# A decoder step with product-key experts: dense gates added element by element with indirect DMAs

## The chip, the core and the metric

One core of a Trainium2 chip runs the whole program in one launch. The metric is the device time of one execution in microseconds (us). Engines: TensorE (PE in the profile), VectorE (DVE), ScalarE (ACT), GpSimd (POOL) and SyncE (SP), which here only issues DMAs. 16 DMA engines move data between HBM and SBUF.

## What is computed

Two blocks in a row on 512 tokens of 1024 features, all float32. The first block is a mixing layer (retention and differential attention) followed by a layer of product-key experts; the second is another attention block. The change is in the experts' layer:

```python
def block(xb):                                     # 128 tokens
    q = (xb @ wq).reshape(t, 8, 2, 128)
    s = jnp.einsum('thpd,hpkd->thpk', q, subkeys)  # 128 keys on each side
    s_top, i_top = lax.top_k(s, 16)
    cand = (s_top[:, :, 0, :, None] + s_top[:, :, 1, None, :]).reshape(t, 8, 256)
    c_top, c_idx = lax.top_k(cand, 16)
    i1 = take(i_top[:, :, 0], c_idx // 16); i2 = take(i_top[:, :, 1], c_idx % 16)
    e = i1 * 128 + i2                              # one of 16384 experts
    g = jax.nn.softmax(c_top, axis=-1)
    act = jax.nn.gelu(einsum('thkd,td->thk', u[e], xb))
    return einsum('thk,thkd->td', g * act, v[e])
```

Each token picks 128 experts (8 heads of 16), each with a gate. Two heads can pick the same expert; its gates then add up.

## The kernel before

The experts' layer is computed densely: `hidden` is gelu(u x) for all 16384 experts and all 512 tokens, and for tokens 128 to 511 (`DENSE` = 3 tiles of 128 tokens, `TD` = 384 tokens) it is multiplied by a dense matrix of gates (zero nearly everywhere) and by v. The first tile of 128 tokens is done by rows instead: GpSimd fetches, for each of the 128 picks, one hidden value (`row_unit`) and one row of v (`row`) per token, and VectorE adds them up.

The stages, in the order of each engine's program:

- Mixing and the scores of the keys (0 to 405 us). GpSimd has nothing to do in it. Weights stream through SyncE's queue in pieces of 512 KB with three buffers.
- The hidden layer (`hidden_*`, 128 blocks j of 128 experts, 405 to 1194 us). For each block SyncE loads a piece of u (L1373, four buffers), ScalarE rounds it to `u_high` (L1420), VectorE subtracts to `u_low` (L1449), TensorE makes 24 products of 128x512 (L1398: high times high, high times low, low times high, for 8 slices), ScalarE applies gelu (L1436), SyncE stores 256 KB to `hidden_scratch` in HBM (L1381). Every third hidden buffer must be stored before it is written again.
- Beside it, in units dealt out by `pace(j)`, runs a background: first the choice of the experts on VectorE (`choose_vector`, four token tiles, tiles 1, 2, 3 and then 0), and behind it, from block 64 on, the building of the gates.
- Building the gates: the picked keys and gates of a tile are transposed on TensorE (L1149, behind a wait for `picked`, L1242 on VectorE) and copied by ScalarE (L1169). Then for each of the 384 tokens VectorE makes a 128x128 one-hot matrix of key 1 (L1345) and two of key 2 times the gate's high and low half (L1347), in float16. TensorE multiplies them (L1290, two products of 128x128 per token, in order between the large products), ScalarE moves four tokens at a time from PSUM into a stage (L1312), and six DMAs of 4 MB store them to `gates_scratch` (L1317), 64 tokens each.
- Combining (`combine_*`, 1194 to 1790 us), 32 groups of four key blocks. SyncE loads the gates of a group (`load_gated`, L1478: six DMAs of 128 KB, L1487, and the hidden values, L1489) and v (L1496, 1 MB each, two a group). VectorE multiplies gates and hidden values (L1635), both factors are split in high and low, and TensorE adds three token tiles up in six PSUM banks (L305 to L307). GpSimd fetches rows and units (L1532, L1539), and VectorE adds them to x (L1657).
- The second block (1790 us to the end), untouched.

The hidden layer and the combining overlap by hand: at the blocks of `EARLY` (116, 119, 121, 123, 125, 127) each engine's program goes one step into its `combine_*`. At block 116 SyncE waits for the gates and calls `load_gated(0)`; this stands in SyncE's program between the store of hidden block 116 and the load of u block 121.

Of the kernel before, what the change touches and what calls it, by code (L numbers as in the profile page):

```python
# [13 lines left out]
P = 128  # L14
T = 512
# [62 lines left out]
class Signals:  # L78


    def __init__(self, nc):
# [28 lines left out]
         self.gate_shifted, self.gate_powered, self.picked, self.picked_turned, self.picked_moved) = semaphores(  # L110
            nc, "subkeys_arrived query_act query_dve keys_scored scores_act scores_dve gate_shifted gate_powered "
                "picked picked_turned picked_moved")

        self.hot_parts, self.gates_built, self.gates_moved = semaphores(
            nc, "hot_parts gates_built gates_moved")
        self.gates_stored = semaphores(nc, "gates_stored0 gates_stored1")
# [265 lines left out]
class Mixing:  # L382
    def __init__(self, m, keep):
# [22 lines left out]
        self.small = region.tensor("mix_small", [P, 64], F32)  # L406
        assert region.at <= keep.stream_at
# [502 lines left out]
GATE_BANKS = (4, 5, 6, 7)  # L910
# [3 lines left out]
GATE_CHUNK = 64  # L914
CHUNKS = TD // GATE_CHUNK
HOT = 16
BLOCKS = TD // HOT
COMBINE_BANKS = (4, 5, 6, 7, 0, 1)
ROWS, UNITS = 8, 16

FIRST_ROW = 10
GATE_SCALE = 2.0 ** 15
BATCH = 4
# [9 lines left out]
def pace(j):  # L933
    return 1 + (j % 4 == 3) if j < 64 else 2
# [12 lines left out]
class Peer:  # L947
    def __init__(self, m, keep):
# [4 lines left out]
        self.chosen = [region.tensor(n, [P, TD], dtype) for n, dtype in (("key1", F16), ("key2", F16), ("gate", F32))]  # L953
# [24 lines left out]
        region = Region(nc, self.scores_at)  # L978
        self.stages = [region.tensor(f"gate_stage{i}", [P, N_KEYS, GATE_CHUNK], F32) for i in range(2)]
        self.every_key = region.tensor("every_key", [P, N_KEYS], F16)  # L980
        self.rounded = region.tensor("gate_rounded", [P, TD], F16)
        self.key_values = [region.tensor(f"key_value{i}", [P, TD], F32) for i in range(2)]
        self.parts = [region.tensor(f"gate_part{i}", [P, TD], F32) for i in range(2)]
        self.hot1 = [region.tensor(f"hot1_{i}", [P, HOT, N_KEYS], F16) for i in range(2)]
        self.weighed = [[region.tensor(f"hot2_part{p}_{i}", [P, HOT, N_KEYS], F16) for p in range(2)] for i in range(2)]

# [7 lines left out]
        hot_end = region.at  # L994
        region = Region(nc, self.scores_at)
        self.gate_in = [region.tensor(f"gate_in{i}", [P, CHUNKS, GROUP, GATE_CHUNK], F32) for i in range(2)]
# [7 lines left out]
        region.at = max(region.at, hot_end)  # L1004
        self.unit_places = region.tensor("unit_places", [P, HK], U32)
        self.row_places = region.tensor("row_places", [P, HK], U32)
        self.row_gate = region.tensor("row_gate", [P, HK], F32)
        self.unit = region.tensor("row_unit", [P, HK], F32)
        self.row_weight = region.tensor("row_weight", [P, HK], F32)
        self.place_value = region.tensor("place_value", [P, HK], F32)  # L1010
        self.place_square = region.tensor("place_square", [P, P], F32)
        self.token = region.tensor("token_number", [P, 1], F32)
# [125 lines left out]
def choose_tensor(m, keep, p):  # L1138
    pe, s = m.pe, m.s
    yield  # L1140
    for t in range(TT):
        for _ in range(CHOICE_STEPS + 6):
            yield
        if t < DENSE:
            b = GATE_BANKS[t % 4]
            pe.wait_ge(s.picked, t + 1)
            m.await_bank(b)
            for i in range(3):
                step = pe.engine.transpose(m.bank[b][:, i * P:i * P + P], p.picked[:, i, :], keep.ident[:, :])  # L1149
            step.then_inc(s.picked_turned, 1)  # L1150
            m.bank_freed[b] = (s.picked_moved, 3 * t + 3)
        yield


def choose_scalar(m, keep, p):
    act, s = m.act, m.s
    yield
    for t in range(TT):
        for _ in range(CHOICE_STEPS):
            yield  # L1160
        act.wait_ge(s.gate_shifted, t + 1)
        act.engine.activation(p.picked[:, 2, :], p.picked[:, 2, :], ACT.Exp).then_inc(s.gate_powered, 1)
        for _ in range(6):
            yield
        if t < DENSE:
            b = GATE_BANKS[t % 4]
            act.wait_ge(s.picked_turned, t + 1)
            for i in range(3):
                act.engine.activation(p.chosen[i][:, t * P:t * P + P], m.bank[b][:, i * P:i * P + P], ACT.Copy).then_inc(s.picked_moved, 1)  # L1169
        yield  # L1170
# [18 lines left out]
def choose_vector(m, keep, p):  # L1189
# [5 lines left out]
    for t in range(TT):  # L1195
# [19 lines left out]
        dve.wait_ge(s.picked_turned, t)  # L1215
# [32 lines left out]
        if t == DENSE:  # L1248
            place_rows(m, keep, p)
# [3 lines left out]
def place_rows(m, keep, p):  # L1253
# [4 lines left out]
    dve.wait_ge(s.picked, TT)  # L1258
    dve.step(v.tensor_tensor(p.place_square[:, :], keep.ident[:, :], keep.counting[:, :], ALU.mult))
    dve.settle()  # L1260
    dve.step(v.tensor_reduce(p.token[:, :], p.place_square[:, :], AX_X, ALU.add))
    dve.step(v.tensor_copy(p.row_gate[:, :], gate))
    dve.settle()
    dve.step(v.tensor_scalar(p.unit[:, :], key1, float(T), p.token[:, :], ALU.mult, ALU.add))
    dve.settle()
    dve.step(v.scalar_tensor_tensor(out=p.place_value[:, :], in0=key2, scalar=float(P * T), in1=p.unit[:, :], op0=ALU.mult, op1=ALU.add))
    dve.settle()
    v.tensor_copy(p.unit_places[:, :], p.place_value[:, :]).then_inc(s.places_ready, 1)
# [9 lines left out]
def gates_tensor(m, keep, p):  # L1278
    pe, s = m.pe, m.s
    for _ in range((1 + 4 + 3) * BATCH):  # L1280
        yield
# [1446 lines left out]
```

## Time and profile before

| | us |
|---|---|
| Runs of the kernel | 2227.22, 2224.61, 2226.02 (median 2226.02) |
| The profiled execution | 2222.24, span of the core 2220.8, mean granted TensorE clock 0.975 |

| engine | busy, us | share of the span |
|---|---|---|
| TensorE | 2075.6 | 93% |
| VectorE | 1451.2 | 65% |
| ScalarE | 760.5 | 34% |
| GpSimd | 357.0 | 16% |

The profile is of one execution. L12 is line 12 of the kernel. A group of instructions is a line, an engine and an operation with its tiles. TensorE's products overlap: a 128x512 product shows some 0.39 us, but the next one starts 0.23 us behind it, so the spacing of blocks is the better measure of its rate. GpSimd's spans are rough.

### The profile page before, as it was taken

Reading aid. Unit: us, or ns where it says so; the run is one execution under the profiler, and the core shown is the slowest. Engines: PE = TensorE matmul, PEld = TensorE weight load, DVE = VectorE, ACT = ScalarE, POOL = GpSimd, SP = SyncE. Lnnn points to the kernel's source line nnn. Section 1 sums busy time; section 2 is a strip of 40 time slices with the busy share of each in tenths; the row PEclk is TensorE's granted clock in tenths of the full one; section 3 lists DMA queues with packets and bytes.
Section 4 is the critical chain, followed back from the end, with each engine's and each line's share of the span. In section 5 each row is a group of like instructions: output and inputs, shape, how many; then the busy total and the mean of one; then the engine's idle time right before and its main releaser. Section 6 shows DMA issues by size and latency. Waiting matters only on the chain.

```text
span 2220.8 us, 25836 instructions
## 1 busy us (share of the span) xinstructions
PE 2075.6 (93%) x9641; PEld 1624.8 (73%) x9641; DVE 1451.2 (65%) x3415; ACT 760.5 (34%) x1101; POOL 357.0 (16%) x262
## 2 busy tenths in 40 slices
PE   6989999999999999999999998889789979999899
PEld 5767778878787866666678886677667757777677
DVE  4465442588787978888823576777668864876434
ACT  4334431333232333333333332222223354334531
POOL 0000000000000000000003557577575200000000
PEclk9999999999999999999999999999899989999999
DMA  5211132244443435555576889899889812221022
GB/s 164 84 57 58 57 105 95 95 133 148 133 143 128 147 123 184 188 184 190 190 290 202 274 287 329 311 320 326 282 305 365 319 50 74 76 76 58 19 96 85
DMA packets 172653, 374.90 MB, mean 169 GB/s; under 512 B 19440, under 2 KB 60912, under 8 KB 171504
## 3 DMA queue, kind: packets, MB, share of 16 engines
q1 hardware_dynamic: 146112, 277.03, 37.4%
q0 software_dynamic: 22528, 67.19, 8.1%
q10 hardware_dynamic: 3888, 29.03, 3.2%
q8 instruction: 76, 1.25, 0.2%
q14 instruction: 49, 0.40, 0.1%
HBM read 312.38 MB, written 60.82 MB: 168 GB/s over the span
## 4 chain that ended last, share of the span: by engine, by line
PE 62%; DVE 15%; DMA 7%; issue 6%; POOL 5%; ACT 5%; SPq 0%; ACTq 0%; DVEq 0%
PE bank L1398 27%; PE bank L305 9%; PE bank L307 9%; PE bank L306 9%; DMA v_raw<-in_peer_v 5%; POOL row_unit L1539 5%; DVE x L1657 2%; PE bank L1290 2%; DVE v_low L1646 1%; DMA row<-in_peer_v,row_places 1%; DVE u_low L1449 1%; DVE hidden_in L1635 1%; PE bank L1949 1%; ACT v_high L1596 1%; DVE weights_low L298 1%
## 5 line engine op out<-in xcount | busy, mean ns | idle before, releaser
L1398 PE MATMUL bank<-xn_low,u_high 128*128 128x512 f32 x1024 | 433.8, 424 | 0.0
L1398 PE MATMUL bank<-xn_high,u_high 128*128 128x512 f32 x1024 | 403.2, 394 | 0.0
L1398 PE MATMUL bank<-xn_high,u_low 128*128 128x512 f32 x1024 | 402.5, 393 | 0.0
L1532 POOL DMA_INDIRECT row<-in_peer_v,row_places x128 | 188.9, 1476 | 1295.3 <-DMA gates_scratch<-gate_stage 1135.5
L305 PE MATMUL bank<-v_high,w_high 128*128 128x512 f32 x768 | 309.9, 404 | 65.1 <-DVE v_low L1646 57.1
L306 PE MATMUL bank<-v_low,w_high 128*128 128x512 f32 x768 | 306.1, 399 | 0.0
L307 PE MATMUL bank<-v_high,w_low 128*128 128x512 f32 x768 | 305.3, 397 | 0.0
L298 DVE TENSOR_TENSOR weights_low<-weights_raw,weights_high 128x1024 fp32r<-128x1024 f32 (+1 forms) x105 | 127.3, 1217 | 231.8 <-ACT weights_high L289 231.6
L1449 DVE TENSOR_TENSOR u_low<-u_raw,u_high 128x1024 fp32r<-128x1024 f32 x128 | 156.4, 1222 | 174.5 <-ACT u_high L1420 174.1
L305 PEld LDWEIGHTS bank<-v_high,w_high 128*128 128x128 f32 x768 | 148.8, 194 | 106.6 <-DVE v_low L1646 67.1
L1398 PEld LDWEIGHTS bank<-xn_high,u_high 128*128 128x128 f32 x1024 | 193.2, 189 | 41.3
L1398 PEld LDWEIGHTS bank<-xn_high,u_low 128*128 128x128 f32 x1024 | 194.9, 190 | 25.3
L1398 PEld LDWEIGHTS bank<-xn_low,u_high 128*128 128x128 f32 x1024 | 194.3, 190 | 25.1
L1347 DVE TENSOR_SCALAR hot_part<-every_key,key_value,gate_part 128x128 f16<-128x128 f16 x768 | 203.7, 307 | 0.0
L1596 ACT ACTIVATE v_high<-v_raw 128x2048 fp32r<-128x2048 f32 x64 | 122.3, 1912 | 226.4 <-DMA v_raw<-in_peer_v 132.4
L1646 DVE TENSOR_TENSOR v_low<-v_raw,v_high 128x2048 fp32r<-128x2048 f32 x64 | 146.4, 2288 | 81.1 <-ACT v_high L1596 53.3
L1657 DVE SCALAR_TENSOR_TENSOR x<-row,row_weight,x 128x1024 f32<-128x1024 f32 x128 | 164.1, 1282 | 45.6 <-DMA row<-in_peer_v,row_places 26.6
L1539 POOL DMA_INDIRECT row_unit<-hidden_scratch,unit_places x128 | 164.4, 1284 | 97.1 <-DMA hidden_scratch<-hidden 58.4
L307 PEld LDWEIGHTS bank<-v_high,w_low 128*128 128x128 f32 x768 | 148.6, 193 | 32.0
L306 PEld LDWEIGHTS bank<-v_low,w_high 128*128 128x128 f32 x768 | 148.9, 194 | 30.6
L1436 ACT ACTIVATE hidden<-bank 128x512 f32<-128x512 f32 x128 | 76.5, 597 | 274.7 <-PE bank L1398 270.7
L289 ACT ACTIVATE weights_high<-weights_raw 128x1024 fp32r<-128x1024 f32 (+1 forms) x105 | 109.7, 1050 | 173.4 <-PE bank L307 171.2
(334 smaller groups left out, 3255.1 us busy)
## 6 DMA issues: line engine op xcount, KB each, us to landing
u_raw<-in_peer_u SPq DMA_DIRECT2D x128, 512.0 KB, 3.7
v_raw<-in_peer_v SPq DMA_DIRECT2D x64, 1024.0 KB
weights_raw<-in_w_in SPq DMA_DIRECT2D x64, 512.0 KB, 3.7
hidden_scratch<-hidden SPq DMA_DIRECT2D x128, 256.0 KB, 2.2
gates_scratch<-gate_stage ACTq DMA_DIRECT2D x6, 4096.0 KB, 13.2
gate_in<-gates_scratch SPq DMA_DIRECT2D x192, 128.0 KB
hidden_in<-hidden_scratch SPq DMA_DIRECT2D x32, 768.0 KB
weights_raw<-in_w_out SPq DMA_DIRECT2D x16, 512.0 KB, 3.6
```

The costliest lines, as they stand in the source:

```text
L298: dve.engine.tensor_tensor(st.part(st.low[n % st.PAIRS], n), st.part(st.raw[n % st.RAW], n), st.part(st.high[n % st.PAIRS], n).bitcast(F32 ...
L305: engine.matmul(out, lh, rh, start=first, stop=False)
L306: engine.matmul(out, lh, rl, start=False, stop=False)
L307: return engine.matmul(out, ll, rh, start=False, stop=last)
L1347: step = v.tensor_scalar(p.weighed[n % 2][half][:, t, :], p.every_key[:, :], key2[:, token], p.parts[half][:, token], ALU.is_equal, ALU.mult)
L1398: step = pe.engine.matmul(m.bank[b][:, :], left[:, k, :], right[:, k, :], start=(done == 0), stop=(done == 3 * KT - 1))
L1449: dve.engine.tensor_tensor(p.u_low[j % U_PAIRS][:, :, :], p.u_raw[j % U_RAW][:, :, :], p.u_high[j % U_PAIRS][:, :, :].bitcast(F32), ALU.su ...
L1532: pool.engine.indirect_dma_start(p.row[i % ROWS][:, :], None, values, bass.IndirectOffsetOnAxis(p.row_places[:, i:i + 1], 0)).then_inc(s.r ...
L1539: pool.engine.indirect_dma_start(p.unit[:, i:i + 1], None, units, bass.IndirectOffsetOnAxis(p.unit_places[:, i:i + 1], 0)).then_inc(s.unit ...
L1596: act.engine.activation(p.v_pair[n % 2][0][:, :, :], p.v_raw[n % 2][:, :, :], ACT.Copy).then_inc(s.v_high, 1)
L1646: v.tensor_tensor(low[:, :, :], p.v_raw[n % 2][:, :, :], high[:, :, :].bitcast(F32), ALU.subtract).then_inc(s.v_low, 1)
L1657: v.scalar_tensor_tensor(out=keep.x[:, 0, :], in0=p.row[i % ROWS][:, :], scalar=p.row_weight[:, i:i + 1], in1=keep.x[:, 0, :], op0=ALU.mul ...
```

## The change

The gates are no longer built. At the start of the program GpSimd clears an 8 KB row per partition and writes it with eight DMAs over the whole scratch tensor `gates` in HBM, now laid out as [key 1, key 2, token] (25 MB, the same size as before). SyncE waits for these before its first load of u. When VectorE has chosen the experts of a dense token tile, it computes each pick's place in that tensor and keeps the gates (`place`, one unit of the background per tile). GpSimd then issues for each of the 128 picks of the tile one indirect DMA that adds 128 gates (one per token) to 128 places in HBM. The places within one DMA differ, since the tokens do. Each 16 DMAs (a head of each token) wait until all adds issued before have landed, since two heads can have the same place. SyncE waits for the last of the 384 before `load_gated(0)`. A group's gates are loaded in one DMA, and the multiplication by them is one instruction. The background on TensorE is gone; VectorE's and ScalarE's ends with the choice, and `pace` stays at five units in four blocks.

```diff
 def pace(j):
-    return 1 + (j % 4 == 3) if j < 64 else 2
+    return 1 + (j % 4 == 3)
...
+        self.nothing = region.tensor("nothing", [P, CLEARED], F32)
+CLEARED, CLEARINGS = 2048, 8
...
-def choose_tensor(m, keep, p):
...
-def gates_tensor(m, keep, p):
...
-def gates_scalar(m, keep, p):
...
-def gates_vector(m, keep, p):
...
+def place(m, keep, p, t):
...
+    dve.wait_ge(s.picked, t + 1)
+    if t == 0:
+        dve.step(v.tensor_tensor(p.place_square[:, :], keep.ident[:, :], keep.counting[:, :], ALU.mult))
...
+    dve.step(v.tensor_copy(p.slot_gate[t][:, :], gate))
+    dve.settle()
+    of_key1, of_key2 = (N_KEYS * TD, TD) if t < DENSE else (T, P * T)
+    number = p.token[:, t % DENSE:t % DENSE + 1]
+    dve.step(v.tensor_scalar(first, key1, float(of_key1), number, ALU.mult, ALU.add))
+    dve.settle()
+    dve.step(v.scalar_tensor_tensor(out=both, in0=key2, scalar=float(of_key2), in1=first, op0=ALU.mult, op1=ALU.add))
+    dve.settle()
...
+        v.tensor_copy(p.slot_place[t][:, :], both).then_inc(s.gates_placed, 1)
+        dve.wait_ge(s.gates_placed, t + 1)
...
+def clear_gates(m, b):
+    pool, s = m.pool, m.s
+    pool.step(pool.engine.memset(b.nothing[:, :], 0.0))
+    pool.settle()
+    keys = N_KEYS // CLEARINGS
+    times = keys * TD // CLEARED
+    for i in range(CLEARINGS):
+        part = m.dram["gates"][:, i * keys:(i + 1) * keys, :].rearrange("a j t -> a (j t)").rearrange("a (n c) -> a n c", c=CLEARED)
+        pool.engine.dma_start(part, b.nothing[:, :].unsqueeze(1).broadcast_to([P, times, CLEARED])).then_inc(s.gates_cleared, 16)
+
+
+def add_gates(m, p):
+    pool, s = m.pool, m.s
+    gates = m.dram["gates"].rearrange("a j t -> (a j t)").rearrange("(n a) -> n a", a=1)
+    pool.wait_ge(s.gates_cleared, 16 * CLEARINGS)
+    for t in range(DENSE):
+        pool.wait_ge(s.gates_placed, t + 1)
+        for i in range(HK):
+            if i % PEER_TOPK == 0 and t + i:
+                pool.wait_ge(s.gates_added, 16 * (t * HK + i))
+            pool.engine.indirect_dma_start(gates, bass.IndirectOffsetOnAxis(p.slot_place[t][:, i:i + 1], 0), p.slot_gate[t][:, i:i + 1], None,
+                                           compute_op=ALU.add).then_inc(s.gates_added, 16)
...
 def hidden_sync(m, keep, p, following):
+    sp.wait_ge(s.gates_cleared, 16 * CLEARINGS)
...
 def combine_sync(m, keep, p):
...
-        for c in range(CHUNKS):
-            sp.engine.dma_start(p.gate_in[at][:, c, :, :], m.dram["gates"][c][:, g * GROUP:(g + 1) * GROUP, :]).then_inc(
-                s.gate_arrived[at], 16)
+        sp.engine.dma_start(p.gate_in[at][:, :, :], m.dram["gates"][:, g * GROUP:(g + 1) * GROUP, :]).then_inc(s.gate_arrived[at], 16)
...
-    sp.wait_ge(s.gates_built, 4 * BLOCKS)
+    sp.wait_ge(s.places_ready, 1)
+    sp.wait_ge(s.gates_added, 16 * DENSE * HK)
     load_gated(0)
...
-        for j in range(GROUP):
-            step = v.tensor_tensor(product[:, j, :, :], product[:, j, :, :], p.gate_in[at][:, :, j, :], ALU.mult)
-        step.then_inc(s.gated, 1)
+        v.tensor_tensor(product, product, p.gate_in[at][:, :, :], ALU.mult).then_inc(s.gated, 1)
...
+    clear_gates(m, b)
+    add_gates(m, p)
     combine_pool(m, p)
```

## Rows read from the trace of the kernel before

**Rows 1.** The page's 40 slices of 55.5 us, busy tenths by engine.
```profile
PE   6989999999999999999999998889789979999899
POOL 0000000000000000000003557577575200000000
DMA  5211132244443435555576889899889812221022
```

**Rows 2.** Windows of the hidden layer: busy time of each engine, granted clock, DMA.
```profile
core 0: us, PE busy (x) PEld busy (x) DVE busy (x) ACT busy (x) POOL busy (x), PEclk, DMA share, GB/s
670.00:783.00 113.00, 113.00 (x494) 93.37 (x492) 90.11 (x311) 34.31 (x46) 0.00 (x0) 0.98 0.41 136
783.00:1120.00 337.00, 337.00 (x1916) 214.91 (x1915) 282.98 (x1153) 127.17 (x191) 0.00 (x0) 1.00 0.49 175
```

**Rows 3.** Timeline of SyncE's issues, 1100 to 1131: start us, us, line.
```profile
1104.12 0.33 SPq L1381 DMA_DIRECT2D hidden_scratch<-hidden  x1
...
1111.16 0.33 SPq L1381 DMA_DIRECT2D hidden_scratch<-hidden  x1
...
1124.44 0.33 SPq L1381 DMA_DIRECT2D hidden_scratch<-hidden  x1
...
1129.88 0.33 SPq L1381 DMA_DIRECT2D hidden_scratch<-hidden  x1
```

**Rows 4.** A window and a wait of the combining stage.
```profile
1340.00:1790.00 450.00, 387.20 (x1607) 311.53 (x1606) 327.93 (x297) 122.44 (x76) 262.27 (x191) 0.94 0.88 315
...
PE bank L305 <- DVE v_low L1646: 57.1, 19, 8.0
```

**Rows 5.** Timeline of SyncE's issues in the combining stage.
```profile
1364.77 7.30 SPq L1487 DMA_DIRECT2D gate_in<-gates_scratch  x6
```

**Rows 6.** Line 1290's own instructions: ns min/median/max, first and last start.
```profile
L1290 PE MATMUL bank<-hot_part,hot x768: 219/224/230, 783.2 to 1120.3; 128*128 128x128 f16 x192
```

**Rows 7.** The picked keys: groups of 405 to 783, VectorE's timeline, a clock window.
```profile
L1149 PE MATMUL bank<-ident,picked 128*128 128x128 f32 x9 | 2.0, 340 | 9.5 <-DVE picked L1242 9.5
...
490.32 2.28 DVE L1242 TENSOR_REDUCE picked<-match 128x128 f32<-128x2048 f32 x1
...
493.00:497.00 4.00, 4.00 (x13) 3.14 (x12) 0.00 (x0) 0.61 (x3) 0.00 (x0) 0.57 0.00 0
```

**Rows 8.** Timelines of SyncE and ScalarE at block 116 and at the end.
```profile
1135.89 2.73 SPq L1487 DMA_DIRECT2D gate_in<-gates_scratch  x6
...
1139.45 1.02 SPq L1373 DMA_DIRECT2D u_raw<-in_peer_u  x1
...
1150.36 1.06 ACT L1420 ACTIVATE u_high<-u_raw 128x1024 fp32r<-128x1024 f32 x1 [4.18 <-DMA u_raw<-in_peer_u]
...
1194.54 0.60 ACT L1436 ACTIVATE hidden<-bank 128x512 f32<-128x512 f32 x1 [3.04 <-PE bank L1398]
```

**Rows 9.** Timelines of GpSimd and VectorE, 1203 to 1213.
```profile
1207.94 0.94 POOL L1539 DMA_INDIRECT row_unit<-hidden_scratch,unit_places  x1 [0.30 <-issue]
...
1210.94 2.03 POOL L1539 DMA_INDIRECT row_unit<-hidden_scratch,unit_places  x1 [0.30 <-issue]
...
1209.87 2.29 DVE L1646 TENSOR_TENSOR v_low<-v_raw,v_high 128x2048 fp32r<-128x2048 f32 x1
```

**Rows 10.** The page's group of the fetches of single elements.
```profile
L1539 POOL DMA_INDIRECT row_unit<-hidden_scratch,unit_places x128 | 164.4, 1284 | 97.1 <-DMA hidden_scratch<-hidden 58.4
```

**Rows 11.** The group of VectorE's u subtractions, 405 to 783.
```profile
L1449 DVE TENSOR_TENSOR u_low<-u_raw,u_high 128x1024 fp32r<-128x1024 f32 x67 | 81.7, 1219 | 73.0 <-ACT u_high L1420 72.5
```

**Rows 12.** The chain of waits: from an indirect load's issue to its use.
```profile
1337.55 5.55 DMA row<-in_peer_v,row_places
...
1656.13 8.19 DMA row<-in_peer_v,row_places
```

**Rows 13.** The chain's start, and two lines of the page's DMA issues.
```profile
2.81 4.23 DMA gain<-in_norm_g
...
weights_raw<-in_w_in SPq DMA_DIRECT2D x64, 512.0 KB, 3.7
...
gates_scratch<-gate_stage ACTq DMA_DIRECT2D x6, 4096.0 KB, 13.2
```

More of the change, by code:

```diff
@@ L952, in __init__ @@
         self.xn_low = region.tensor("xn_low", [P, KT, T], F32R)
-        self.chosen = [region.tensor(n, [P, TD], dtype) for n, dtype in (("key1", F16), ("key2", F16), ("gate", F32))]
+        self.slot_gate = [region.tensor(f"slot_gate{i}", [P, HK], F32) for i in range(TT)]
+        self.slot_place = [region.tensor(f"slot_place{i}", [P, HK], U32) for i in range(TT)]
+        assert region.at <= keep.rows_at + 36864
         region.at = keep.rows_at + 36864
@@ L1247, in choose_vector @@
         yield
-        if t == DENSE:
-            place_rows(m, keep, p)
+        place(m, keep, p, t)
         yield
-def place_rows(m, keep, p):
+def place(m, keep, p, t):
     dve, s = m.dve, m.s
@@ L1257, in place_rows @@
     key1, key2, gate = (p.picked[:, i, :] for i in range(3))
-    dve.wait_ge(s.picked, TT)
-    dve.step(v.tensor_tensor(p.place_square[:, :], keep.ident[:, :], keep.counting[:, :], ALU.mult))
+    first, both = (tile[:, :] for tile in p.place_value)
+    dve.wait_ge(s.picked, t + 1)
+    if t == 0:
+        dve.step(v.tensor_tensor(p.place_square[:, :], keep.ident[:, :], keep.counting[:, :], ALU.mult))
+        dve.settle()
+        dve.step(v.tensor_reduce(p.token[:, 0:1], p.place_square[:, :], AX_X, ALU.add))
+        dve.settle()
+        for i in range(1, TT):
+            dve.step(v.tensor_scalar(p.token[:, i:i + 1], p.token[:, 0:1], float(i * P), None, ALU.add))
@@ L1393, in hidden_tensor @@
         m.await_bank(b)
[L1395 removed]
         for k in range(KT):
[L1397 to L1408 removed]
+            step = three_products(pe.engine, m.bank[b][:, :], (high[:, k, :], low[:, k, :]),
+                                  (p.xn_high[:, k, :], p.xn_low[:, k, :]), k == 0, k == KT - 1)
+        step.then_inc(s.hidden_summed, 1)
+        m.bank_freed[b] = (s.hidden_out, j + 1)
         if j in EARLY:
@@ L2605, in tensor_program @@
 def tensor_program(m, keep, b, p, w):
-    def background():
-        for _ in choose_tensor(m, keep, p):
-            for _ in range(BATCH):
-                yield
-        yield from gates_tensor(m, keep, p)
     mixing_tensor(m, keep, b)
     combining = combine_tensor(m, keep, p)
-    hidden = hidden_tensor(m, keep, p, background(), combining)
+    hidden = hidden_tensor(m, keep, p, combining)
     scores_tensor(m, keep, p, hidden)
@@ L2629, in scalar_program @@
     combining = combine_scalar(m, keep, p)
-    hidden = hidden_scalar(m, keep, p, background(), combining)
+    hidden = hidden_scalar(m, keep, p, choose_scalar(m, keep, p), combining)
     scores_scalar(m, keep, p, hidden)
@@ L2646, in vector_program @@
     combining = combine_vector(m, keep, p)
-    hidden = hidden_vector(m, keep, p, background(), combining)
+    hidden = hidden_vector(m, keep, p, choose_vector(m, keep, p), combining)
     scores_vector(m, keep, p, hidden)
```

184 lines of the change are left out of this document (19 added, 165 removed).

## The prediction

> **What bounds the kernel now.** I read the page's slices first [rows 1]: TensorE is at nine tenths or more through nearly the whole middle of the run, GpSimd does nothing before slice 21, and the DMA engines are at four to five tenths while the hidden layer runs and at eight to nine in the combining stage. So there are two regimes, and the change touches both.
>
> In the hidden layer (about 405 to 1194 us) the windows show TensorE busy without a gap from 670 to 1120 [rows 2]. How fast it goes is read from SyncE's stores of the hidden rows, one per key block j: while gates are built they lie 7.04 us apart (1104.12 to 1111.16), and behind the gates 5.44 us (1124.44 to 1129.88) [rows 3]. The difference, 1.60 us a block, is the 16 small gate products among 24 large ones.
>
> In the combining stage the DMA engines are the nearer limit: from 1340 to 1790 TensorE is busy 387 of 450 us at a mean granted clock of 0.94, against a DMA share of 0.88, and TensorE waits 57.1 us for v_low [rows 4]. SyncE cannot even issue there: six small gate loads took it 7.30 us [rows 5].
>
> **What the change removes from TensorE.** 768 gate products (384 tokens by two) [rows 6] go, and 8 tokens a block cost 1.60 us, so 48 blocks give 48 x 1.60 = 77 us. They stand on the path: no idle time lies beside them. The nine transposes of the picked keys go as well. TensorE stood 9.5 us idle for them, three times about 3.2, while VectorE reduced the picked keys, and behind the first one the granted clock fell to 0.57 of full over 4 us, which is 1.7 us lost [rows 7]. Three times (3.2 + 1.7) is 15 us. Check: 128 blocks at 5.44 are 696 us, 405 + 696 = 1101, against the last hidden eviction at 1194.54 [rows 8]; 93 us, the same as 77 + 15. What is late next is VectorE, which has to split each u block. It is busy 90 of 113 us before 783 [rows 2], that is 4.5 us a block where 5.44 are given, and the placing arithmetic adds some six short instructions, about 2 us, per token tile of 15 blocks. I take 2 us of the gain away: the hidden layer could end 91 us earlier, at about 1103. From ScalarE and VectorE the evictions and 1152 one-hot rows go; both lie beside TensorE and are worth nothing.
>
> **What it adds on GpSimd, and who waits for it.** 384 indirect DMAs of 128 single elements, in 24 batches of 16; a batch starts only when the one before has landed. The first tile's places are ready when the reduce at 490.32 is over (492.6 us) plus one VectorE unit in the next block, about 498 [rows 7]. The other two tiles follow some 88 us apart and are never what GpSimd waits for, if a batch is over 11 us.
>
> SyncE waits for the last add before it loads the first gates. In the kernel before that point is 1135.89 [rows 8]; 91 us earlier it is 1045. Behind this wait on SyncE stand all further u loads and hidden stores. The u load next in line was issued at 1139.45 and used by ScalarE at 1150.36, so from release to use 14.5 us, plus 1.05 for ScalarE's split and 1.22 for VectorE's: 16.8 us. TensorE still has four loaded blocks (4 x 5.44 = 21.8 us, counted from about 1 us before the release point), so the cover is only 4 us. Adds that land by 1049 cost nothing, later ones one for one. When they land at F, seven blocks are left to compute behind the 16.8 us, with 2 us for a cold clock: the hidden layer ends at F + 16.8 + 38.1 + 2 = F + 57.
>
> Cost of a batch: 15 instructions with the gap behind each, then the last one's landing, then 0.3 us. No row of before shows an adding DMA or an indirect write. The nearest is the gather of single elements (row_unit): bare 0.94 us with a 0.30 us gap, but 2.03 when it began (1210.94) under a long VectorE subtraction (1209.87 for 2.29 us) [rows 9]; 1.284 on average [rows 10]. In the hidden layer VectorE has such an instruction 1.22 us in every 5.6 [rows 11], so a GpSimd instruction meets one with chance 0.22 for half of 1.22 us: 0.13 us. So a gather would be 1.07 there; I take 1.15 for an add, nearer to the gather than to the blocked one, because an add has one more read. Landing: an indirect load was in use 5.55 us after its issue in one place and 8.19 in another, under heavier DMA traffic [rows 12]. I take 6.0, near the lower, since the hidden layer's traffic is half, with something for the read of the destination. A batch is then 15 x 1.45 + 6.0 + 0.3 = 28.05 us. Below: 15 x 1.24 + 5.1 + 0.3 = 24.0 (bare instructions, landing a little under the shorter row). Above: 15 x 1.58 + 8.2 + 0.3 = 32.2.
>
> F = 498 + 24 x 28.05 = 1171, 122 us behind the point at which TensorE starts to starve. The hidden layer ends at 1228 instead of 1194.5: **+33.5 us**. All of the 91 us is eaten, and a third more.
>
> The Trainium skill ("DMA: Bandwidth & Descriptors", Specifications) says that below 512 B the DMA engines do a read-modify-write; every element here is 4 B. No row here shows its price, and nothing above uses it; it speaks for the upper end.
>
> **What it adds at the start.** 25 MB of zeros in eight GpSimd DMAs in the first 100 us. The six gate stores of 4 MB, the same bytes, landed in 13.2 us each, so they need some 80 us of the DMA engines. The weight stream takes a 512 KB piece every 5.5 us (24 large products) with three buffers; halved bandwidth turns its 3.7 us to landing into about 8, which three buffers cover. What has no cover is the very start, where the chain runs through the small gain loads (4.23 us) and x [rows 13]. Between nothing (all is there before the first zero moves) and 20 us (each load doubled); I take 6, as the memset and the issue come about 3 us in, when most loads are under way. **+6 us.**
>
> **The combining stage.** The gate loads go from six of 1 KB rows to one of 6 KB rows per group, same bytes; the multiplication goes from four instructions to one. VectorE's part is hidden. On DMA, the 25 MB take about 77 us at the stage's mean rate, and larger rows save perhaps a sixth, 13 us, while SyncE issues 160 DMAs fewer. The stage is near its DMA limit, so most of it counts: between 0 and 60 (all of TensorE's waits), I take **-12 us**, the DMA saving and no more.
>
> Sum: 33.5 + 6 - 12 = +27.5. The profiled execution took 2222.24 us for a span of 2220.8; that gives 2250. The median of the runs shown, 2226.02, is 4 us above it, which is less than the error of any term; I forecast **2251**.
>
> **The rivals.** In a batch of B us the change is 24 x B - 645.5 us; it decides at B = 26.9.
> - Adds late, but quicker than I think (B 23 to 26.7): a landing of 4 to 5 us in the light traffic of the hidden layer and instructions at 1.07. For it speaks that 1.07 is what the rows give for a gather. At B = 25.5: -33, 2192. The Trainium skill ("DMA: Bandwidth & Descriptors", Anatomy of one DMA) puts the fixed part of a GpSimd DMA at about 2.0 us; by it B would be 24.1, -67 us, 2159. The rows of an indirect load, 5.55 and 8.19 us, do not agree with it.
> - Adds in time (B under 22.9): 2226 - 91 + 6 - 12 = 2129. Needs bare instructions and a landing of 4 us at once; against it the blocked gathers.
> - Adds far dearer than gathers (B from 33): were the instruction 2.03 us, as the blocked one, B is 15 x 2.33 + 6.3 = 41.3, +346, 2572; at B = 35, 2420. For it: one more read per element and no row that excludes it.
> - The start costs its 20 us: 14 more on any of these.
>
> **How the numbers follow.** Forecast (B 27.1 to 33) 0.44, around 2251, from 2231 to 2372; late but quick 0.27; in time 0.08; far dearer 0.14; in the gap between 0.07. Slower by over 0.2% (4.4 us, about what a measurement of this kernel tells from no change) is 0.44 + 0.14 = 0.58; faster 0.27 + 0.08 = 0.35; same 0.07. The range goes from B = 24.0 (24 x 24.0 - 645.5 = -70, 2156) down a little to 2150, and from B = 32.2 (+127, 2353) up to 2365; the in-time case and most of the dear one lie outside, some 2 in 10.
>
> **What will show it.** Hidden stores 5.44 us apart from the first block to block 116, no L1149 wait; then a gap of some 120 us on TensorE near 1055 with SyncE waiting for the last add, and a fall of the granted clock behind it. GpSimd busy without pause from 498 to about 1170, an add at about 1.15 us, each sixteenth followed by some 6 us of idle. First matmul later by about 6 us. TensorE busier from 1340 on, DMA share down. The forecast is wrong if a batch is under 27 us or the gap is missing; if VectorE cannot keep 5.44 us a block beside the choosing; or if the zeros delay the first stage by tens of us.

## The result and the profile after

The changed kernel takes 2386.4 us (median of 4 runs, 2382.0 to 2391.3) against 2226.6 for the kernel before: 1.0716 times as long, interval 1.0696 to 1.0737. The forecast was 2251 with a range up to 2365. The profiled execution took 2384.51 us for a span of 2383.2, 162.4 us more than the span of before, at a mean granted clock of 0.926 (before 0.975).

From the page of after: slices (now of 59.6 us), the group of the adds, and a line of its DMA issues.

```profile
PE   6989999999999999991000699988988988899899
...
POOL 1000000037787777777777174757767400000000
PEclk9999999999999999995555799989999999999999
DMA  9611222356666666652222588889988951222032
...
L1267 POOL DMA_INDIRECT gates_scratch<-slot_gate,slot_place x384 | 620.5, 1616 | 684.5 <-DVE slot_place L1239 501.2
...
gates_scratch<-nothing POOLq DMA_DIRECT2D x8, 3072.0 KB, 50.0
```

Against [rows 1] there is a hole: in slices 20 to 22 TensorE does nothing, from slice 19 to 22 the clock granted to it is at 0.5 of full (1.2 GHz), and GpSimd works at seven tenths. The other three tenths are the gap of 0.30 us behind every instruction and the waits for landings. The first DMA slice has gone from 5 to 9. An add takes 1616 ns on average, where a gather took 1284 [rows 10].

SyncE's waits of after (line, what it waited for: us in all, times, longest), then its timeline at block 116, where the loads stop and start again:

```profile
SPq L50 <- DMA gates_scratch<-slot_gate,slot_place: 257.6, 1, 257.6
...
1041.29 0.33 SPq L1290 DMA_DIRECT2D hidden_scratch<-hidden  x1
...
1046.73 0.33 SPq L1290 DMA_DIRECT2D hidden_scratch<-hidden  x1
...
1052.17 0.33 SPq L1290 DMA_DIRECT2D hidden_scratch<-hidden  x1
...
1057.61 0.33 SPq L1290 DMA_DIRECT2D hidden_scratch<-hidden  x1
...
1315.69 0.33 SPq L1383 DMA_DIRECT2D gate_in<-gates_scratch  x1
...
1316.55 0.50 SPq L1280 DMA_DIRECT2D u_raw<-in_peer_u  x1
```

The hidden blocks are 5.44 us apart up to the last one, as the blocks behind the gates were [rows 3]. Then comes one wait of 257.6 us, and no load of u is issued in it: the next one comes 0.86 us after the release.

GpSimd's timeline at the end of a batch, one add that VectorE holds up, the last batch's start, and the last add (start us, duration, and in brackets the idle time before it and what ended it):

```profile
539.74 1.54 POOL L1267 DMA_INDIRECT gates_scratch<-slot_gate,slot_place  x1 [0.30 <-issue]
545.15 1.54 POOL L1267 DMA_INDIRECT gates_scratch<-slot_gate,slot_place  x1 [3.87 <-DMA gates_scratch<-slot_gate,slot_place]
...
1058.57 1.23 DVE L1348 TENSOR_TENSOR u_low<-u_raw,u_high 128x1024 fp32r<-128x1024 f32 x1 [4.21 <-ACT u_high L1319]
...
1058.63 2.57 POOL L1267 DMA_INDIRECT gates_scratch<-slot_gate,slot_place  x1 [0.30 <-issue]
...
1284.90 1.54 POOL L1267 DMA_INDIRECT gates_scratch<-slot_gate,slot_place  x1 [1.74 <-DMA gates_scratch<-slot_gate,slot_place]
...
1312.61 1.54 POOL L1267 DMA_INDIRECT gates_scratch<-slot_gate,slot_place  x1 [0.30 <-issue]
```

A bare add is 1.54 us, and a batch of 16 took (1315.69 - 510.33) / 24 = 33.56 us on average from the first add to SyncE's release. Here 15 x (1.616 + 0.30) = 28.74 us are the instructions, and 4.82 us go from the issue of the last one to the next. In single batches that is 5.41 us beside the hidden layer's traffic (539.74 to 545.15) and 3.28 us when nothing but the adds moves (1281.62, the add before, to 1284.90). The Trainium skill ("DMA: Bandwidth & Descriptors", Anatomy of one DMA) gives some 2.0 us as the fixed part of such a DMA. From its issue even the quiet landing is longer here; from the end of its instruction (1.74 us) it is near that figure.

The start, in windows (us; busy time and count of PE, PEld, DVE, ACT, POOL; clock, DMA share, GB/s), and ScalarE's wait before 110 us:

```profile
24.00:100.00 76.00, 69.71 (x290) 55.28 (x289) 23.39 (x25) 21.26 (x27) 0.00 (x0) 0.96 0.94 381
1057.00:1315.00 258.00, 21.71 (x96) 17.64 (x94) 2.45 (x2) 3.68 (x5) 201.87 (x131) 0.55 0.22 1
...
ACT weights_high L286 <- DMA weights_raw<-in_w_in: 46.3, 12, 8.1
```

In the same first window TensorE had 74.50 us of work before, at a DMA share of 0.38, and ScalarE waited for no weights. Now the share is 0.94, ScalarE waits 46.3 us for pieces of the weights, and the first hidden eviction comes at 425.95 instead of 411.07 us.

### The profile page after: what moved, and what is told of

It is laid out like the page before. It is cut to its first block, busy times and chain, and to the rows that moved or that the text cites. A ratio compares the mean times of both kernels' runs of the same rounds, so it can differ in the third digit from the quotient of the medians.

```text
span 2383.2 us, 23059 instructions
## 1 busy us (share of the span) xinstructions
PE 1999.0 (84%) x8864; PEld 1625.9 (68%) x8864; DVE 1212.0 (51%) x2176; ACT 705.2 (30%) x996; POOL 985.5 (41%) x655
## 3 DMA queue, kind: packets, MB, share of 16 engines
q0 software_dynamic: 81024, 92.58, 17.0%
q8 instruction: 70, 1.15, 0.2%
## 4 chain that ended last, share of the span: by engine, by line
PE 30%; POOL 29%; DMA 13%; DVE 11%; issue 11%; ACT 5%; SPq 0%; ACTq 0%; DVEq 0%; POOLq 0%
POOL gates_scratch L1267 24%; PE bank L302 9%; PE bank L304 9%; PE bank L303 9%; DMA v_raw<-in_peer_v 5%; POOL row_unit L1435 4%; DMA gates_scratch<-slot_gate,slot_place 4%; DMA weights_raw<-in_w_in 3%; DVE x L1548 2%; DMA row<-in_peer_v,row_places 1%; DVE v_low L1537 1%; DVE weights_low L295 1%; DVE hidden_in L1527 1%; POOL row L1428 1%; ACT w_high L1495 1%
## 5 line engine op out<-in xcount | busy, mean ns | idle before, releaser
L1267 POOL DMA_INDIRECT gates_scratch<-slot_gate,slot_place x384 | 620.5, 1616 | 684.5 <-DVE slot_place L1239 501.2
L302 PE MATMUL bank<-xn_high,u_high 128*128 128x512 f32 x1024 | 399.7, 390 | 251.2 <-DVE u_low L1348 251.2
L303 PE MATMUL bank<-xn_low,u_high 128*128 128x512 f32 x1024 | 399.3, 390 | 0.0
L302 PE MATMUL bank<-v_high,w_high 128*128 128x512 f32 x768 | 308.5, 402 | 56.2 <-DVE v_low L1537 56.1
L295 DVE TENSOR_TENSOR weights_low<-weights_raw,weights_high 128x1024 fp32r<-128x1024 f32 (+1 forms) x105 | 127.4, 1217 | 244.3 <-ACT weights_high L286 244.0
L1319 ACT ACTIVATE u_high<-u_raw 128x1024 fp32r<-128x1024 f32 x128 | 134.7, 1053 | 259.8 <-DMA u_raw<-in_peer_u 259.8
L1435 POOL DMA_INDIRECT row_unit<-hidden_scratch,slot_place x128 | 168.5, 1317 | 95.1 <-DMA hidden_scratch<-hidden 56.4
```

Of the source, the lines that this page charges most:

```text
L295: dve.engine.tensor_tensor(st.part(st.low[n % st.PAIRS], n), st.part(st.raw[n % st.RAW], n), st.part(st.high[n % st.PAIRS], n).bitcast(F32 ...
L302: engine.matmul(out, lh, rh, start=first, stop=False)
L303: engine.matmul(out, lh, rl, start=False, stop=False)
L1267: pool.engine.indirect_dma_start(gates, bass.IndirectOffsetOnAxis(p.slot_place[t][:, i:i + 1], 0), p.slot_gate[t][:, i:i + 1], None, compu ...
L1319: act.engine.activation(p.u_high[j % U_PAIRS][:, :, :], p.u_raw[j % U_RAW][:, :, :], ACT.Copy).then_inc(s.u_high, 1)
L1435: pool.engine.indirect_dma_start(p.unit[:, i:i + 1], None, units, bass.IndirectOffsetOnAxis(p.slot_place[DENSE][:, i:i + 1], 0)).then_inc( ...
```

## The experiments

All compare with runs of the kernel before on the same chip (medians 2220.6 to 2225.9). `ratio` is to that kernel, with its 95% interval. Times with no other count are medians of four runs. The kernels with fewer adds or elements, or with writes in place of adds, leave part of the gates out.

**Two tiles.** Are the late adds the whole loss, and is the rest of the sum right?

```diff
-    for t in range(DENSE):
+    for t in range(ADDED):                     # ADDED = 2
...
-    sp.wait_ge(s.gates_added, 16 * DENSE * HK)
+    sp.wait_ge(s.gates_added, 16 * ADDED * HK)
```

> The adds of the third dense token tile are left out (256 of 384 indirect adds; SyncE waits for these 256), so the gates of 128 tokens stay zero. My theory: the changed kernel loses its time only because the adds land late. In its trace a batch of 16 takes 33.55 us (805.3 us from the first add at 510.3 to SyncE's release at 1315.7, over 24), so 16 batches land at 1047, 11 us before SyncE stores hidden block 116 (1057.6); TensorE never stops, the hidden layer ends near 1117 instead of 1371, and the time is 2386 - 254 = 2132 us. Rival: the gain of the hidden layer is eaten elsewhere (GpSimd's or the DMA engines' work slows the combining once nothing stalls): above 2170. Rival two: adds in flight slow the blocks themselves: stores of hidden rows further apart than 5.44 us.

Measured 2129.4 us (2126.9 to 2135.1), ratio 0.9568 [0.9546, 0.9590]. A window and SyncE's timeline:

```profile
420.00:1057.00 637.00, 637.00 (x2812) 527.61 (x2811) 356.78 (x1052) 193.89 (x248) 417.05 (x255) 1.00 0.60 144
...
1056.20 0.33 SPq L1291 DMA_DIRECT2D hidden_scratch<-hidden  x1
1061.19 0.33 SPq L1384 DMA_DIRECT2D gate_in<-gates_scratch  x1
```

With 256 adds in place of 384, TensorE is busy in all of 637 us, and the hidden layer takes 690.9 us (424.5 to 1115.4), which is 127 x 5.44. Before it was 783.5 (411.07 to 1194.54). So the gate products and the picked keys are worth 92.6 us (I had 93, less 2 for VectorE, which costs nothing). The last add lands at 1061, not at the 1047 that was expected: from the first add at 508.9 a batch takes 34.5 us beside the hidden layer, and 33.56 is the mean with the quicker batches of the hole. SyncE waits 4.5 us for it, and TensorE waits for nothing; I had put this cover at 4 us. 257 us of the changed kernel's time, then, come with the third tile's adds.

**Plain writes.** What part of an add is the adding? The same DMAs write the gates instead of adding them, so that of two equal picks one is lost.

```diff
-            ..., None, compute_op=ALU.add).then_inc(s.gates_added, 16)
+            ..., None).then_inc(s.gates_added, 16)
```

> The same 384 indirect DMAs with plain writes instead of adds (experts picked by two heads of a token keep one gate only). Theory one, the read and add are what made an instruction 1.54 us where a gather's was 0.94: an instruction of about 0.95 us, a batch of 15 x 1.25 + 6 = 25 us, the last lands at 510 + 24 x 25 = 1110, the hidden layer ends near 1167, 2386 - 204 = 2182 us. Rival, it is the direction (an indirect write, whatever it computes, costs 1.54): 2386 us and no change in the instruction. The landing behind each batch (some 3.2 us of idle with the adds) tells the same for the DMA engines' part.

The instruction is 0.96 us (384 of them, 956/962 ns min and median), as short as the gather, and behind a batch GpSimd goes on 1.46 us after the end of the last one. The time is another matter: 2340 to 2561 us in four runs, which scatter so much that I take no time from it, only what the profile of one of them (2459.8 us) shows. SyncE's stores of the hidden rows, a window, TensorE's products in the middle of a block, all of ScalarE's waits for u, and a window in which GpSimd mostly waits for the second tile's places:

```profile
516.92 0.33 SPq L1289 DMA_DIRECT2D hidden_scratch<-hidden  x1
533.20 0.33 SPq L1289 DMA_DIRECT2D hidden_scratch<-hidden  x1
571.90 0.33 SPq L1289 DMA_DIRECT2D hidden_scratch<-hidden  x1
637.00 0.33 SPq L1289 DMA_DIRECT2D hidden_scratch<-hidden  x1
...
508.00:800.00 292.00, 159.42 (x547) 111.08 (x546) 98.48 (x382) 35.23 (x45) 169.07 (x171) 0.70 0.19 59
...
594.36 0.58 PE L302 MATMUL bank<-xn_high,u_high 128*128 128x512 f32 x1 [2.22 <-issue]
597.16 0.58 PE L303 MATMUL bank<-xn_low,u_high 128*128 128x512 f32 x1 [2.22 <-issue]
599.26 0.58 PE L304 MATMUL bank<-xn_high,u_low 128*128 128x512 f32 x1 [1.52 <-issue]
...
ACT u_high L1318 <- DMA u_raw<-in_peer_u: 0.5, 1, 0.5
...
690.00:756.00 66.00, 65.60 (x286) 53.03 (x285) 61.51 (x197) 22.27 (x29) 11.73 (x11) 1.00 0.46 154
```

Soon after the first write (508.19) the blocks are 16, 39 and 65 us apart, while the DMA share is 0.19. It is not that loads of u come late: ScalarE waits for one 0.5 us in all. What is late is TensorE's own program. In the middle of a block, where the kernel makes it wait for nothing, its products start mostly 2.1 to 2.8 us apart in place of 0.23, and the profile shows nothing that they waited for. From 682 to 741, where GpSimd issues no write, TensorE is at full rate again (65.60 of 66 us busy from 690 to 756). So a write is cheap for GpSimd and dear for TensorE beside it, though the DMA engines are far from full; by what way it holds TensorE up no run here shows. Theory one's 2182 is missed, by something that neither theory named.

**Plain writes, slower.** Is it the rate? Each pair of writes waits for the pair before. (The expectation takes the blocks' delay for late loads of u; the rows above show that it is not.)

```diff
-            if i % PEER_TOPK == 0 and t + i:
+            if i % 2 == 0 and t + i:
...
-            ..., None, compute_op=ALU.add).then_inc(s.gates_added, 16)
+            ..., None).then_inc(s.gates_added, 16)
```

> Plain writes in place of adds as in the run of writes only, but each pair of DMAs waits until the one before has landed, so there are fewer element writes per us (about 2.6 us for a DMA in place of 1.27, slower than the adds at 2.1). In the run without this u loads arrived 15 to 64 us late while the writes went on (DMA share 0.05 to 0.16) and the time was 2340 to 2561 us. Theory: plain 4-byte writes pile up behind their semaphores when they come faster than they are absorbed; at this rate they don't: no u load late, adds' place taken by writes until 510 + 192 x 5.2 = 1508, so SyncE is released 193 us later than in the changed kernel: 2580 us, with blocks 5.44 us apart up to 1057. Rival: any plain 4-byte write in HBM holds the loads up, at any rate: blocks far more than 5.44 us apart from 510 on.

Measured 2461.5 us (two runs, 2456.8 and 2466.1), ratio 1.1089 [1.1035, 1.1144]. The same window, and the page's line of GpSimd's queue (packets, MB, share):

```profile
508.00:800.00 292.00, 292.00 (x1290) 241.88 (x1289) 226.09 (x754) 90.42 (x116) 118.96 (x110) 1.00 0.46 146
...
q0 software_dynamic: 38016, 92.58, 10.1%
```

TensorE is busy in all 292 us. Sixteen writes in a row, 0.96 + 0.30 = 1.26 us apart, hold it up; pairs of them, 2 x 2.30 us from pair to pair ((1390.8 - 509.4) / 384 = 2.30 us a write), don't. The time is long only since a pair took 4.6 us, and it is under the forecast since I had it at more. The packets differ from those of the adds as well: 81024 with adds, 38016 with plain writes, 43008 fewer or 112 a DMA. With half the elements (next run) the adds show 56448, which is 24576 or 64 a DMA fewer than 81024: an add sends each element in a packet of its own. If what else belongs to a DMA is the same in both, that leaves a plain write 128 - 112 = 16 packets, eight elements in each. The edit changes two things at once, the rate and the number of writes under way (at most two in place of 16), and no run parts them. The adds, with up to 16 under way at 1.85 us each, hold nothing up. That packing plays a part is possible and not shown.

**Half the elements.** Does an add cost by the element or by the instruction? Only partitions 0 to 63 add their gates.

```diff
-            ..., IndirectOffsetOnAxis(p.slot_place[t][:, i:i + 1], 0), p.slot_gate[t][:, i:i + 1], None,
+            ..., IndirectOffsetOnAxis(p.slot_place[t][0:64, i:i + 1], 0), p.slot_gate[t][0:64, i:i + 1], None,
```

> The changed kernel with 384 adds of 64 elements each (the gates of the other 64 tokens of every dense tile are left out). It asks what the 1.54 us of an adding instruction scale with. Theory: with the elements (an add needs more descriptors per element than a gather's 0.94 or a plain write's 0.96): about 1.0 us, a batch 16 x 1.05 + 4.5 + 3 = 24.3 us, the last add lands at 510 + 583 = 1093, hidden layer to 1150 in place of 1371, 2165 us. Rival: it is fixed per instruction, then 1.5 us and 2380 us.

Measured 2326.4 us (two runs, 2325.8 and 2327.1), ratio 1.0481 [1.0451, 1.0511]. The adds' own row (ns min/median/max):

```profile
L1267 POOL DMA_INDIRECT gates_scratch<-slot_gate,slot_place x384: 1410/1419/3279, 509.2 to 1252.7; - x192
```

64 elements take 1.42 us where 128 take 1.54: 0.12 us for 64 elements and, by a straight line through these two (an estimate), some 1.3 us whatever their number. The 60 us that are gained are 39.5 of instructions (384 x 0.103) and some 20 of landings. The cost is nearly all fixed per instruction, so the fixed case (2380) was right of the instruction; the 54 us under it are its small part by the element, and the landings.

**Interleaved.** How much is the wait for landings? The heads of the three tiles are dealt in turn, with one semaphore for each tile: two tiles never have the same place.

```diff
+ADD_ORDER = (0, 0, 0, 1, 0, 1, 0, 2, 1, 0, 2, 1, 0, 2, 1, 0, 2, 1, 2, 1, 2, 1, 2, 2)
...
-    for t in range(DENSE):
+    for t in ADD_ORDER:
+        head = done[t]
...
+        if head:
+            pool.wait_ge(s.gates_added[t], 16 * head * PEER_TOPK)
```

> All adds, the same work, but batches of different token tiles alternate where they can, with one semaphore for each tile, so that a batch waits for the last one of its own tile, which landed during another tile's. Theory: the landing waits (23 of about 3.2 us, of them 3 left) go and nothing else changes: the adds end 60 us earlier, 2386 - 60 = 2326 us. Rival: the adds are bound by the DMA engines behind GpSimd, so GpSimd's instructions grow longer or the waits come back: within 10 us of 2386.

Measured 2324.6 us (2322.2 to 2327.1), ratio 1.0442 [1.0425, 1.0460]. From the rows of the adds' idle time, after first and then interleaved:

```profile
  DMA gates_scratch<-slot_gate,slot_place: 55.9, 23
```

```profile
L1272 POOL DMA_INDIRECT gates_scratch<-slot_gate,slot_place x384: 1541/1542/3631, 507.8 to 1249.4; - x192
...
  issue: 115.9, 380
  DMA gates_scratch<-slot_gate,slot_place: 7.7, 3
```

The waits go from 55.9 to 7.7 us (and 11.5 us of them had been put down to issue, 127.4 before), and the adds end some 61 us earlier (1249.4 against 1312.6, begun 2.5 us earlier). All of it arrives at the end of the kernel, -61.8 us, since SyncE's wait is still 196.9 us long.

**Clearing later.** Is it the zeros that delay the start? GpSimd begins to clear behind the last step of the first weight stream, at 90 us.

```diff
 def clear_gates(m, b):
+    pool.wait_ge(s.multiplied, m.stream.summed("diff_v", 3))
```

> The eight clearing DMAs are issued only when the third weight group (diff_v) is multiplied, near 90 us, where the weight stream has pauses. Theory: the 15 us by which the hidden layer starts later (420.4 for 405.3) are ScalarE's waits for weight pieces beside the zeros (46 us of them up to 110 us, none before), and they vanish: 2386 - 14 = 2372 us. Rival: the zeros cost the same wherever they are, since attention's loads stand beside them then: 2386. The adds are unchanged at 33.5 us a batch in both.

Measured 2369.9 us (2365.7 to 2373.5), ratio 1.0651 [1.0633, 1.0668], 16.5 us less. The same windows:

```profile
24.00:100.00 76.00, 74.50 (x330) 61.11 (x329) 28.80 (x46) 25.22 (x37) 6.30 (x8) 1.00 0.47 150
100.00:200.00 100.00, 90.40 (x410) 71.19 (x409) 61.07 (x130) 36.17 (x89) 0.00 (x0) 0.95 0.71 283
```

TensorE is back at its 74.50 us, ScalarE waits for no weights before 110 us, the first hidden eviction is at 413.6, and the first add at 498.0, where I had put it. The 2.5 us that are left against 411.1 are no more than runs differ in a stretch that nobody changed (3.6 in the kernel before with one load, below). So the same bytes from 90 us on cost nothing that shows.

**Both.** Do the two gains add up?

> All 384 adds, with both repairs: batches of different token tiles alternate, and the zeros are written from 90 us on. If the two act on different stretches they add up: 2386.4 - (2386.4 - 2324.6) - (2386.4 - 2369.9) = 2308 us. If one had only moved the other's wait, 2320 or more. Either way above the kernel before (2226): the bare price of 384 instructions of 1.54 + 0.30 us, 709 us, ends the adds at 498 + 709 + 13 = 1220, where SyncE is at 1042.

With both edits 2310.6 us (2303.2 to 2315.3), ratio 1.0368 [1.0343, 1.0393]: 75.8 us less, where the two alone give 61.8 + 16.5 = 78.3. They add up within the runs' spread. It is still slower than before: SyncE waits 197.0 us.

**The kernel before with one load.** Is the layout alone worth the 12 us of the combining stage? Gates are built as before but stored as [key 1, key 2, token], loaded in one DMA and multiplied in one instruction.

```diff
-        for c in range(CHUNKS):
-            sp.engine.dma_start(p.gate_in[at][:, c, :, :], m.dram["gates"][c][:, g * GROUP:(g + 1) * GROUP, :])...
+        sp.engine.dma_start(p.gate_in[at][:, :, :], m.dram["gates"][:, g * GROUP:(g + 1) * GROUP, :])...
```

> The kernel before (gates by one-hot products), only with the changed layout of the gates in HBM: six stores in pieces of 256 B, and one load of 6 KB rows a group in place of six of 1 KB. Theory: the combining stage is 12 us shorter (from the last hidden eviction to the first addition of the last outputs 599.5 us before, 587.2 in the changed kernel, 588.0 with two tiles) because of the loads alone, so 2226 - 12 = 2214, if the scattered stores (hidden beside the blocks) cost nothing. Rival: the 12 us come from something else in the changed kernel (a later start, less left in the queues), so 2226; or the stores in pieces cost more than they give, above 2226.

Measured 2216.9 us (six runs, 2215.0 to 2221.8), ratio 0.9969 [0.9946, 0.9992], a gain of 0.3%. From the last hidden eviction to the first sum of a bank into x it is 587.4 us (1202.5 to 1789.9) against 599.5 before (1194.54 to 1793.98). The 12 us are there; part is given back in the hidden layer, which ends 8 us later. 3.6 of these 8 us are already there when it begins, where the kernel had not been changed, so I don't lay them to the edit. The other 4.4 us come with the gate stores, now in pieces of 256 B. Their issue, SyncE's wait for the last of them at block 116, and TensorE's wait behind that:

```profile
gates_scratch<-gate_stage ACTq DMA_DIRECT2D x6, 4096.0 KB, 26.6
...
SPq L50 <- DMA gates_scratch<-gate_stage: 10.5, 1, 10.5
...
PE bank L1398 <- DVE u_low L1449: 3.0, 1, 3.0
```

A store lands in 26.6 us where it took 13.2 [rows 13]. The kernel before has neither of the two waits. Of the 10.5 us 3.0 get through to TensorE, and its granted clock is 0.98 from 1120 to 1202, where it was 1.00 before; that is 1.6 us more (an estimate, 0.02 of 82 us).

**Four loads.** Is it the size of the rows or the number of loads? The kernel with two tiles, with four loads of 1.5 KB rows in place of one of 6 KB.

```diff
-        sp.engine.dma_start(p.gate_in[at][:, :, :], m.dram["gates"][:, g * GROUP:(g + 1) * GROUP, :])...
+        for c in range(GROUP):
+            sp.engine.dma_start(p.gate_in[at][:, c, :], m.dram["gates"][:, g * GROUP + c, :])...
```

> As the kernel with two tiles of adds (2129.4 us), but a group's gates are loaded by four DMAs of 1.5 KB rows instead of one of 6 KB rows. Theory: the rows' size and the number of issues on SyncE's queue are what gives the 12 us; with 1.5 KB rows most of them go: 2137 to 2141. Rival: neither matters, it is the single multiplication on VectorE (1.6 us for 2.0): 2129.

Measured 2135.6 us (2131.4 to 2136.5), ratio 0.9594 [0.9578, 0.9610], which is 6.2 us over its twin by the medians, though the twin ran on another chip and the two intervals overlap; the stage itself takes 590.8 us against 588.0 by the profiles. So at most half of the 12 us comes back with four loads, and perhaps none. What the rest hangs on (rows from 1 to 1.5 KB, two issues, one multiplication) stays open.

**Two tiles added, the third built.** The runs so far say that GpSimd has time for 256 adds and not for 384, and that 128 tokens of products cost TensorE a third of 77 us. So tiles 1 and 2 are added (cleared late), and the third is built by one-hot products as before, into a tensor of its own. This computes everything.

```diff
-    for t in range(DENSE):
+    for t in range(ADDED):                     # in add_gates
...
+        sp.engine.dma_start(p.gate_in[at][:, :, 0:TA], m.dram["gates"][:, group, :])...
+        sp.engine.dma_start(p.gate_in[at][:, :, TA:TD], m.dram["gates_built"][:, group, :])...
...
-    sp.wait_ge(s.gates_added, 16 * DENSE * HK)
+    sp.wait_ge(s.gates_added, 16 * ADDED * HK)
+    sp.wait_ge(s.gates_built, 4 * BLOCKS)
+    sp.wait_ge(s.gates_stored, 16)
```

> Two token tiles by adds (256, cleared from 90 us on) and the third by one-hot products, stored once in an 8 MB tensor of its own; all of the computation is there. Theory, with the prices measured: 16 batches of 33.5 us from 498 end at 1034, before SyncE needs them; TensorE pays 128 tokens at 0.20 us (26 us) and one wait for picked keys (5 us) instead of 77 + 15; the hidden layer ends at 405 + 696 + 31 = 1132 instead of 1194.5, and combining takes 12 us less with two loads a group: 2226 - 62 - 10 = 2154 us. Rival: what two tiles of adds leave is taken by VectorE, which now has the choosing, the placing and the one-hot rows with GpSimd in its way: 2180 or more.

Measured 2171.5 us (median of 5 runs, 2157.1 to 2173.1), ratio 0.9755 [0.9738, 0.9771]. It beats the kernel before by 54 us and the changed one by 215. SyncE's timeline at block 116, and TensorE's longest wait in the hidden layer:

```profile
1081.59 0.33 SPq L1424 DMA_DIRECT2D hidden_scratch<-hidden  x1
1082.17 0.38 SPq L1528 DMA_DIRECT2D gate_in<-gates_scratch  x1
...
PE bank L1441 <- DVE u_low L1492: 4.1, 1, 4.1
```

There is no wait at block 116, though with little to spare: the last add begins at 1060.8, 21 us ahead. (The 1034 expected for it took 33.5 us a batch, which beside the hidden layer is too little, as with two tiles.) VectorE, the rival's worry, makes TensorE wait 4.1 us once for u_low and 3.5 us once for the picked keys. The hidden layer ends at 1140.8 and the combining takes 589.7. The profiled execution is the fastest of the five, at 2157.1 and near the forecast of 2154; the other four are at 2170 to 2173. What these 14 us are no profile here shows.

## Why the prediction was wrong in size, step by step

The direction, the mechanism and the place were right; the time lies outside the range. Measured against the sum (times from the profiles):

| term | predicted | measured |
|---|---|---|
| gate products and picked keys gone | -93 | -92.6 (two tiles) |
| VectorE's share of it | +2 | 0 |
| an add, on average | 1.15 | 1.616 |
| last add's issue to the next batch | 6.3 | 4.82 |
| a batch of 16 | 28.05 | 33.56 |
| first add | 498 | 510.3 (495.5 less the late start of 14.9; 498.0 measured with clearing later) |
| last add landed to the last hidden eviction | 57 | 55.2 (1315.7 to 1370.9) |
| start | +6 | +14.9 |
| combining | -12 | -12.3 (599.5 to 587.2) |

- **The step that failed is the price of the adding instruction**, a term that was mis-sized. I took 1.15 us, by the gather; it is 1.54 bare. That is 15 x 0.47 = 7.0 us a batch, less 1.5 us for a landing that I had too long: 5.5 us, 24 times, **132 us**. What the choice rested on was "one more read", added to a gather; the plain write shows that the gather's figure does hold for a write (0.96 against 0.94), and that the adding form costs 0.58 us more. By the run with half the elements only some 0.25 of its 1.54 us go with them (an estimate), so most of the 0.58 is not a read for each element. Why it is dearer is open. I left 2.03 us, the dearest row that I had [rows 9], out of the range and in a rival with 0.14; the bound above should have been it.
- **The formula held**: 24 x 33.56 - 645.5 = +160 us, or 2382 on the profiled execution's 2222. (The forecast counts from 2222 and the rivals from 2226, a difference of 4 us that decides nothing.) So this is the rival of far dearer adds (B from 33), just past its lower end.
- **The start** was the second miss, 9 us. I argued that three buffers cover the weights because a piece's landing would go from 3.7 to 8 us. But the eight clearing DMAs are queued at once, so the DMA engines are at 0.94 and not at half, and the wait comes in twelve pieces of up to 8.1 us; moving them away takes it back (clearing later).
- These two are the miss: 27.5 predicted + 132 + 9 = 168.5, and the small terms (first add -2.5, hidden end -1.8, combining -0.3, second block -1.7) take it to 162, the spans' difference. The hidden end is early since the cover was 6.4 us (SyncE waited 257.6, TensorE 251.2) and not 4.
- **VectorE holding up GpSimd** was sized well: 0.13 us an add predicted. From 510 to 1057 us an add took 419.20 / 255 = 1.644 us, 0.10 over the bare one; from 1062 to 1312, where VectorE makes one instruction, it took 195.58 / 127 = 1.540. The add at 1058.63 began 0.06 us behind a subtraction of 1.23 and took 2.57. The Trainium skill ("SBUF — State Buffer", Who interferes with whom) says that a VectorE instruction with two inputs in SBUF contends with a GpSimd instruction that reads SBUF, and the trace agrees: 1.54 us plus nearly the rest of the subtraction.
- **The rule on small elements** that I named as speaking for the upper end ("DMA: Bandwidth & Descriptors" of the Trainium skill, Specifications: a read-modify-write below 512 B) does not explain the miss by itself: the plain writes have the same 4 B, and their instruction is 0.96 us.
- **The combining** came out at -12.3, and the kernel before with one load shows the same 12.1 without any add. The number has luck in it: that larger rows save a sixth I took from no row, and that they are the reason is not settled (four loads). TensorE stands idle 56 us in the stage and stood so 65, but its wait for v_low is the same (56.1 and 57.1 us), and the DMA share hardly falls (0.86 and 0.87).
- What would show it: the spacing of 5.44, the missing L1149 wait, the single wait of SyncE and the low clock behind it are all there; but an add is at 1.62 and not 1.15 us, and the hole on TensorE has twice the length forecast, 251.2 us.

## What to carry to other kernels

When work moves to GpSimd's DMAs, count instructions first: 384 of them at 1.85 us, issue gap included, are 710 us, and no landing that is hidden changes that. An indirect DMA's price is taken from one of the same form, not from the nearest gather; where there is none, the dearest row stands in the range. A split by the engines' free time (two tiles here, one there) can win where either way alone doesn't, and a large fill at the start belongs behind the first stage's loads.

## What the runs showed of the chip that I had not expected

- An indirect DMA that adds takes GpSimd 1.54 us for 128 elements and 1.42 for 64; one that writes 128 takes 0.96, one that fetches them 0.94.
- In one profile, with up to 16 element writes following each other every 1.26 us, TensorE's products started 2.1 to 2.8 us apart over long stretches with nothing to wait for, at a DMA share of 0.19. Writes in pairs, 2.30 us each, held up none, and adds every 1.85 us none either.
- An add sends each 4 B element as a packet, 112 packets more per DMA than a plain write.
- Stores of 4 MB landed in 26.6 us with pieces of 256 B, where they took 13.2 in the old layout.
- Eight clearing DMAs of 3 MB, issued at once, took the DMA share from 0.38 to 0.94 and made a stream of 512 KB pieces wait 46.3 us.
